# A fifteenth load place in the expert stage of a two-layer encoder, for one of its four places of rounded upper parts

## What is computed

```python
h = rmsnorm(x, g_mix[i]);  z = h @ w_in[i]
u, q, k, v = jnp.split(z, splits, axis=-1)
y_ssm = ssm_mixer(u, ...);  y_att = diff_attention(q, k, v, ...)
x = x + jnp.concatenate([y_ssm, y_att], axis=-1) @ w_out[i]
h = rmsnorm(x, g_ffn[i])
# layer 0
x = x + swiglu(h, dense_w_gate, dense_w_up, dense_w_down)
# layer 1
logits = h @ w_router + b_router
top_vals, top_idx = lax.top_k(logits, 2);  top_w = softmax(top_vals)
for e in range(8):
    out = out + gates[:, e:e + 1] * ((silu(h @ w_gate[e]) * (h @ w_up[e])) @ w_down[e])
# at the end
return rmsnorm(x + out, g_final)
```

## Time and profile before

| | |
|---|---|
| median of 3 runs | 1451.57 us (1449.51 to 1459.04) |
| the profiled execution | 1450.17 us, of which the span of the trace is 1448.3 us |
| mean granted TensorE clock | 0.977 of full speed |
| expert stage | from 598 us to the end |
| busy | PE 1360.8 us (94%), VectorE 872.9 us, ScalarE 691.2 us |
| transfers | 435.58 MB, 301 GB/s over the span |

### The profile page before, as it was taken

The page is one execution under the profiler, slowest core; times in us unless marked ns, Lnnn a source line. Parts: engine busy times, 40 slices in busy tenths (PEclk is TensorE's granted clock), DMA queues, the critical chain, the costliest instruction groups (busy, mean ns, idle before and its releaser), DMA issues.

```text
span 1448.3 us, 19121 instructions
## 1 busy us (share of the span) xinstructions
PE 1360.8 (94%) x7254; PEld 981.7 (68%) x7254; DVE 872.9 (60%) x1112; ACT 691.2 (48%) x1023; POOL 135.4 (9%) x111
## 2 busy tenths in 40 slices
PE   6996889999899779799999999999999999999997
PEld 5865558888787555666676666676666766666763
DVE  6888754554388875665555565655656555566552
ACT  4578443434246863344454434544444454444441
POOL 0455200000005640000000000000000000000000
PEclk9997999999899889799999999999999999999999
DMA  8541325453363125599999999999999999999993
GB/s 336 173 175 34 125 109 209 176 176 139 146 222 117 62 92 227 205 403 398 408 420 420 421 420 420 407 420 420 420 421 420 408 419 421 420 420 421 420 421 138
DMA packets 66329, 435.58 MB, mean 301 GB/s; under 512 B 8192, under 2 KB 14720, under 8 KB 16576
## 3 DMA queue, kind: packets, MB, share of 16 engines
q1 hardware_dynamic: 64848, 429.60, 73.8%
q0 software_dynamic: 1392, 4.78, 0.9%
HBM read 429.11 MB, written 2.10 MB: 298 GB/s over the span
## 4 chain that ended last, share of the span: by engine, by line
PE 81%; DVE 8%; ACT 4%; DMA 4%; issue 2%; SPq 0%; ACTq 0%; DVEq 0%
PE ps L2165 21%; PE ps L2201 13%; PE ps L2151 10%; PE ps L2052 7%; PE ps L2183 6%; PE ps L1819 6%; PE ps L2031 4%; PE ps L1957 2%; DMA last_ring<-wmoe 2%; PE ps L1934 2%; DMA mixw<-wmix 1%; PE ps L2287 1%; DVE raw L1301 1%; PE ps L1857 1%; PE ps L1945 1%
## 5 line engine op out<-in xcount | busy, mean ns | idle before, releaser
L2052 PE MATMUL ps<-wsplit,xh 128*128 128x512 f32 (+1 forms) x352 | 111.5, 388 | 5.0 <-DVE hv L1368 3.4
L1630 DVE TENSOR_TENSOR hv<-hv,ps 128x256 f32<-128x256 f32 x56 | 23.6, 421 | 125.9 <-ACT hv L966 125.9
L1378 DVE TENSOR_TENSOR low_raw<-raw,first_uppers 128x2048 fp32r<-128x2048 f32 x36 | 82.2, 2289 | 24.3 <-ACT first_uppers L816 24.1
L1819 PE MATMUL ps<-hT,mixw 128*128 128x256 f32 x384 | 89.9, 395 | 3.3 <-DMA mixw<-wmix 3.3
L1378 DVE TENSOR_TENSOR low_raw<-raw,last_uppers 128x2048 fp32r<-128x2048 f32 x33 | 75.3, 2288 | 24.8 <-ACT last_uppers L816 24.8
L2201 PE MATMUL ps<-raw,hn 128*64 128x256 f32 x768 | 89.7, 383 | 0.0
L1342 DVE TENSOR_TENSOR wsplit<-raw,wsplit 128x2048 fp32r<-128x2048 f32 x33 | 74.5, 2289 | 20.1 <-ACT wsplit L775 20.1
L1819 PEld LDWEIGHTS ps<-hT,mixw 128*128 128x128 f32 x384 | 75.5, 199 | 15.5 <-issue 2.2
L959 ACT ACTIVATE hv<-ps 128x128 f32<-128x128 f32 x56 | 15.5, 277 | 146.7 <-PE ps L2215 146.7
L966 ACT ACTIVATE hv<-ps 128x256 f32<-128x256 f32 x56 | 21.5, 384 | 133.7 <-PE ps L2165 133.7
L2165 PE MATMUL ps<-first_uppers,tokens_next 128*128 128x512 f32 x240 | 79.2, 411 | 2.4 <-DVE low_raw L1378 1.8
(11 more groups left out here) (355 smaller groups left out, 3086.4 us busy)
## 6 DMA issues: line engine op xcount, KB each, us to landing
raw<-wmoe SPq DMA_DIRECT2D x148, 1024.0 KB, 18.5
first_ring<-wmoe SPq DMA_DIRECT2D x94, 1024.0 KB, 19.0
last_ring<-wmoe SPq DMA_DIRECT2D x92, 1024.0 KB, 18.8
raw<-wdense SPq DMA_DIRECT2D x33, 1024.0 KB, 5.1
mixw<-wmix SPq DMA_DIRECT2D x12, 2048.0 KB, 8.3
cyt<-bmat SPq DMA_DIRECT2D x2, 2048.0 KB, 14.4
cw<-cmat SPq DMA_DIRECT2D x2, 2048.0 KB, 23.4
qk<-wglu SPq DMA_DIRECT2D x2, 1024.0 KB, 5.1
```

The source lines that it names most:

```text
L1378: tt(lows[at], ring[at], uppers[k % UPPERS].bitcast(F32), ALU.subtract).then_inc(s["lo_done"], 1)
L1819: ins = mm(ps[:, bank(u), j * 256:j * 256 + 256], mixw[:, c % 2, f, n * P:(n + 1) * P], hT[:, f, :], start=(f == 0), stop=(f == KT - 1))
L2052: ins = mm(to, x2[:, fx, t * P:(t + 1) * P], of, start=(fx == 0 and i == 0), stop=(fx == KT - 1 and i == 2))
```

## The change

A load place takes the room of one upper place. `PLACES` goes from 14 to 15 and `UPPERS` from 4 to 3, and the new place is the tile `spare`, with its lower part `low_spare` on the same bytes. With it 17 heavy pieces are loaded ahead rather than 16: load 14 goes to `spare`, load 15 to `once`, both after the output projection, and load 16 to `hT` after the logits.

With three upper places the split of B(1), which is piece k = 3, must wait until A(0) is done, and ScalarE can't wait for that before it has moved the first tokens. So its part of the split of B(1) goes from ahead of the router's softmax to behind the two `gather_half`. The split of D(0), k = 4, must now wait until B(0) is done, and `silu(0)` is put ahead of it. From then on ScalarE's order is as before; only the count that each split waits for is one higher. Nothing is changed in PE's and VectorE's order.

```diff
-PLACES = 14
+PLACES = 15
 ONCE = 2
-UPPERS = 4
+UPPERS = 3
...
-        sb("uppers_behind", [P, 2, PIECE], F32R)
+        sb("upper_behind", [P, PIECE], F32R)
+        low_spare = sb("low_spare", [P, PIECE], F32R)
...
-        last_uppers = sb("last_uppers", [P, 2, PIECE], F32R)
+        last_upper = sb("last_upper", [P, PIECE], F32R)
+        spare = sb("spare", [P, PIECE])
...
-        ring += [once[:], hT[:].rearrange("p f t -> p (f t)")]
-        lows += [tokens_next[:].rearrange("p k f t -> p (k f t)"), low_hT[:]]
+        ring += [spare[:], once[:], hT[:].rearrange("p f t -> p (f t)")]
+        lows += [low_spare[:], tokens_next[:].rearrange("p k f t -> p (k f t)"), low_hT[:]]
...
-        uppers = [first_uppers[:, 0], first_uppers[:, 1], last_uppers[:, 0], last_uppers[:, 1]]
+        uppers = [first_uppers[:, 0], first_uppers[:, 1], last_upper[:]]
...
             load_piece(14, 0)
+            load_piece(15, 0)
             sp.wait_ge(s["lg_done"], 1)
-            load_piece(15, 0)
+            load_piece(16, 0)
...
                     split("A", 1)
-                    split("B", 1)
...
                     if c == 0:
+                        split("B", 1)
+                        silu(0)
                         split("D", 0)
...
-                    silu(c)
+                    if c:
+                        silu(c)
```

## The result

The changed kernel takes 1459.22 us in the median of 20 runs (1457.19 to 1467.83), and before, run beside it 20 times, 1451.05 us (1447.55 to 1460.74). The ratio is 1.006 with a 95% interval of 1.0045 to 1.0074, that is 6.5 to 10.7 us more. It stays within 1%, but it is clear of noise and four times the rise that was forecast (2.1 us), and the median lies 0.2 us above the stated range. The profiled execution took 1459.92 us, with a span of 1458.0 us against 1448.3.

What follows compares the result with a forecast made beforehand. The prediction took saturated weight transfers as the bound, with PE within 5 us. S of 5.3 us less 3.2 gave +2.1 us, so 1452.3 on the profile or 1453.7 on the median; forecast 1453, range 1446.5 to 1459 us.

Steps and rivals of the forecast that it cites:

- The gain row: Load VectorE waits for, beside the added load at 575 us; delay taken as 0, rival 2.5 us later, chance 0.1.
- The first hole in the transfers: Low transfer rate from 611 to 615 us, 33 GB/s; forecast to grow by some 4 to 5 us.
- S: PE's lateness at the expert stage's start: 3.55 us stall plus 1.75 us for the clock, 5.3 us.
- the second hole: Lower transfer rate from 670 to 680 us, 315 and 374 GB/s; forecast to be there still.
- S - 3.2: Shift of the end of the transfers, with two loads fewer (5.0 us) behind the second hole; +2.1 us.
- the size of the clock's fall: Behind PE's longer pause at the stage start, 3.5 us at half speed were to lose 1.75 us.
- who made PE's waits: PE's 4.7 us of waits from 640 to 1400 us were read as pieces landing late, so PE alone would end sooner.
- S - 4.7: Shift of PE's own limit, its waits taken as room; +0.6 us, so the transfers stayed the later limit.
- The sum: Transfers +2.1 us, PE alone +0.6 us, the later one setting the end; chance 0.45.
- The one with a bare stall: Rival: the clock holds at the stage start, S is 3.55 us and the end moves by +0.4 us; chance 0.2.
- The one on held ScalarE: Rival: three upper places hold ScalarE at D(c)'s split in every chunk, over 1% slower, 1467.5 us at 0.4 each; chance 0.06.

Runs made afterwards that it cites:

- e1: Changed kernel with VectorE's order at the stage start edited: rank tables and matrix, lower part of B(1), product(0), lower part of D(0); 1448.67 us, ratio 1.0008.
- e2: As e1, but with 14 load places instead of 15, still three upper places; 1448.76 us, ratio 0.9992.
- e5: e1 plus, in chunks 47 and 53, the next A piece's split ahead of silu on ScalarE and ahead of product on VectorE; 1444.96 us, ratio 0.9971.
- e6: As e5, but with 14 load places; 1446.50 us, ratio 0.997.
- e7: Kernel before (14 load places, 4 upper places) with only e5's edit of chunks 47 and 53; 1445.99 us, ratio 0.9969.
- e4: Changed kernel with 15 unused matmuls on PE between A(1) and the wait for product(0); 1451.70 us, ratio 1.0015.
- e8: Changed kernel with VectorE's rank tables and matrix ahead of the lower part of B(1), product(0) not moved; 1456.81 us, ratio 1.0027.
- e3: Changed kernel with 14 load places, so the stall without the added place; 1458.70 us, ratio 1.0062.

## Why the prediction was wrong

**Right, by its own steps.** VectorE starts the lower part of B(1) late (3.46 us of idle time), `product(0)` comes 3.5 us later against the start of the stage, and PE's pause is 3.75 us, each as worked out. The gain row was not moved by the added load (6.43 us of wait for it, and 6.6 before). The first hole in the transfers grew from 4 us to 12 (stretches under 100 GB/s: 611 to 615 before, 612 to 624 changed), by about S and not by 4 to 5 us, since S was larger. The first load behind the second hole went out at 681.99 us, where 673.2 + S gives 681.6 with the measured S of 8.4 us, and the end of the transfers followed S - 3.2 (5.2 against 5.4). ScalarE waits for no matmul ahead of a split in the later chunks. No chunk behind the start lost time to three upper places: e1 and e2 run with three and are within 0.25% of before at either end of their intervals.

**First step that failed: the size of the clock's fall.** I took 1.75 us, from the stretch of 3.5 us at 0.52 in rows 8, between 0 (the clock holds) and 3.7 (the light gather taking twice its 3.68 us of rows 7). It was 4.8 us, beyond my upper bound. The lower clock lasted 10.3 us here, with PE busy in all of them, over the whole light gather and most of B(1), and I had let the bound end with the gather. S was 8.4 us and not 5.3.

The trace of the kernel before already had longer stretches, and I passed over them. One stands behind a pause of 2.73 us, shorter than the one to be priced:

```profile
389.82 3.67 PE L1804 MATMUL ps<-cst,hn 128*128 128x128 f32 x16 [2.73 <-DVE hn L1114]
389.00:399.00 10.00, 7.66 (x26) 6.49 (x27) 6.13 (x23) 6.36 (x15) 0.00 (x0) 0.50 0.98 415
```

The other stands behind PE's wait for the routing. PE took up work again at 589.47 us, and the gather of the first heavy tokens (L2379) still ran at 0.50 up to 597 us (columns: stretch, length, PE, PEld, clock, DMA share, GB/s):

```profile
592.00:597.00 5.00, 5.00 (x23) 5.00 (x24) 0.50 0.00 0
```

At a clock of 0.50 such stretches of 8 to 10 us lose 4 to 5 us. That is an estimate from these rows, and the 4.8 us lie in it. Why the stretch is 3.5 us in rows 8 and 8 to 10 us elsewhere no run here shows; the length of the pause doesn't order them.

**Second step that failed: who made PE's waits.** I read 4.7 us of waits for lower parts as waits for late transfers and took them as room: PE's own pace would swallow that much of a delay. Only 0.9 us were. The other 3.7 us, which go in e5, e6 and e7, are waits that the order makes at chunks 47 and 53, and they come again however late PE is. So PE's limit moved by S - 0.9 and not S - 4.7, and it lies behind the S - 3.2 of the transfers. In the kernel before, the transfers hold PE up at 1223 and 1239 us, by 0.9 us together, and in the changed kernel nowhere. ScalarE's waits for transfers behind 625 us fell from 32.0 us to 5.6. The fifteenth place had given the transfers 3.2 us, of which at most 0.9 could show.

**A term that was missing: a second fall of the clock.** The sum had nothing for the waits near 1300 and 1380 us beside their own length. In the profiled execution of the changed kernel the clock fell to 0.50 behind one of them, which costs about 1.7 us by the next row.

**The sum again.** PE's limit is S - 0.9, plus 1.7 us where the clock falls once more for 3.4 us behind one of the two waits (half of the 3.4 us at 0.50; an estimate), as it did in this execution:

```profile
1307.80:1311.20 3.40, 3.40 (x11) 2.68 (x10) 3.07 (x3) 0.00 (x0) 0.00 (x0) 0.50 1.03 422
```

For the changed kernel that is 8.4 - 0.9 + 1.7 = 9.2 us, and its stage is 9.1 us longer. For e4 it is 3.6 - 0.9 = 2.7 against 2.8. For e1, whose S is -0.4, it is -0.4 - 0.9 + 1.7 = 0.4 against 0.4. For e8, where the clock fell near 1304 us too (3.4 us at 0.50), it is 5.7 - 0.9 + 1.7 = 6.5 against 6.5. For e7 the order's waits go instead, -3.7 against -3.7. Five executions are met within 0.2 us. e5 is met less well, with -0.4 - 0.9 - 3.7 = -5.0 against -5.5. The kernels with 14 places and three upper places keep waits for transfers (1.1 us in e2, 0.4 in e3, 1.1 in e6); with these in place of the 0.9 the same sum gives -0.3 against -0.3 for e2, 9.6 against 9.3 for e3 and -3.9 against -4.0 for e6. All of these terms were read from one execution of each kernel after the result, so this is an account of the traces and not a test. How often the late fall comes, and how much of the scatter of the runs it makes, I can't say from one profile of each kernel.

Of the rivals, none had this outcome. The one with a bare stall had the delay of e4 (3.6 us), but not its time: it gave +0.4 us, and e4's stage is 2.8 us longer. The one on held ScalarE didn't occur. The loss came by my own path, with the price of the clock too small and the slack of PE too large. That the time stayed within 1% of before, to which I gave 0.92, doesn't support the sum; the stage is 9.1 us longer where the sum had 2.1.

## What to carry to other kernels

When an operation is delayed on one engine, look at what stands behind it in the order of the next one. Here eight small operations, a selection matrix and a product were dragged along by a split that only B(1) needed. With the first two ahead of that split on VectorE, and the product ahead of the next one (e1), no loss is left that the runs resolve. Before a wait is counted as slack, ask what released the instruction it waited for: here the waits that the order makes were paid again in full, and only the waits for late transfers gave way. And a pause of PE can have a second price in the clock: behind 3.75 us it was 4.8 us, behind 2.67 us it was 3.2.

The lowest median is that of e5, with three upper places, 15 load places and both orders changed, 5.0 us under before; its interval ends just below 1.0 (0.9999). The edit of chunks 47 and 53 alone (e7) gives 3.9 us by the medians, and the runs don't resolve the difference between the two.

## What the runs showed of the hardware that I had not expected

Fifteen matmuls whose result nobody reads, put in a pause of PE, made the kernel 5.8 us faster by the medians, each set against its own before (8.2 us over 1451.05 without them, 2.4 us over 1449.30 with them). They cost PE next to nothing, since it would have waited (0.33 us of the wait are left behind them), and the granted clock stayed at 1.00.

The granted clock fell behind pauses of 3.75 and 2.67 us, behind each at the start of the stage (0.50 over 10.3 us, and 0.66 over the 10 us of the window). Behind PE's waits of 1.8 to 1.9 us near 1300 and 1380 us it fell in some executions (changed, e1, e3, e8: once each, to 0.50 for 3.3 to 3.4 us) and in others it stayed at 1.00 (before, e2, e4).
